# Pair-wide value products with the values as weights, in the stick-breaking and forget attentions of a three-layer transformer kernel

## The reference, cut to what matters

```python
# stick breaking, query tile i of 128 rows, keys 0..q1
z = einsum('bhqd,bhkd->bhqk', q[:, :, q0:q1], k[:, :, :q1]) * scale
strict = pos[:q1][None, :] < pos[q0:q1][:, None]
log_keep = where(strict, log_sigmoid(-z), 0.0)
log_rest = cumsum(log_keep, axis=3, reverse=True) - log_keep
a = where(strict, exp(log_sigmoid(z) + log_rest), 0.0)
out = einsum('bhqk,bhkd->bhqd', a, v[:, :, :q1])
# forget attention, the same tiles
logits = einsum('bhqd,bhkd->bhqk', q[:, :, q0:q1], k[:, :, :q1]) * scale
logits = logits + cum_log_f[:, :, q0:q1, None] - cum_log_f[:, :, None, :q1]
p = softmax(where(causal, logits, -inf), axis=-1)
out = einsum('bhqk,bhkd->bhqd', p, v[:, :, :q1])
# both: merged heads times silu(gate), then times their part of w_out
```

## Time and profile before

| what | value |
|---|---|
| median of 3 runs | 2019.23 us (2018.88 to 2021.91) |
| the profiled execution | 2014.13 us |
| its span, first to last instruction | 2012.3 us |
| PE busy | 1937.3 us, 96% of the span |
| PE weight loads busy | 1582.5 us |
| DVE / ACT / POOL busy | 773.2 / 885.8 / 661.5 us |
| mean granted PE clock | 0.992 |
| chain that ended last | PE 85%, DVE 7%, ACT 4%, issue 3% |

### The profile page before, as it was taken

The page is one execution under the profiler, slowest core; times in us unless marked ns, Lnnn a source line. Parts: engine busy times, 40 slices in busy tenths (PEclk is TensorE's granted clock), DMA queues, the critical chain, the costliest instruction groups (busy, mean ns, idle before and its releaser), DMA issues.

```text
span 2012.3 us, 25999 instructions
## 1 busy us (share of the span) xinstructions
PE 1937.3 (96%) x9707; PEld 1582.5 (79%) x9719; DVE 773.2 (38%) x1393; ACT 885.8 (44%) x1741; POOL 661.5 (33%) x278
## 2 busy tenths in 40 slices
PE   8998999999999899999999999999999999999998
PEld 6887787877788778787776788888778878888886
DVE  3435655444543565544446672010360431111002
ACT  4555565344455555534453742332453343323222
POOL 2422232321233232232122444434203424444442
PEclk9999999999999999999999999999999999999999
DMA  4221222212322122222132232223102423333232
GB/s 151 84 74 43 74 64 63 74 63 74 115 74 74 53 63 64 64 74 63 70 141 65 92 95 94 92 86 94 64 1 74 136 74 95 101 97 94 95 100 88
DMA packets 44573, 163.82 MB, mean 81 GB/s; under 512 B 6192, under 2 KB 6448, under 8 KB 43824
## 3 DMA queue, kind: packets, MB, share of 16 engines
q1 hardware_dynamic: 42640, 148.65, 23.4%
q10 hardware_dynamic: 1824, 13.63, 1.8%
HBM read 155.97 MB, written 6.29 MB: 81 GB/s over the span
## 4 chain that ended last, share of the span: by engine, by line
PE 85%; DVE 7%; ACT 4%; issue 3%; DMA 0%; POOL 0%; DVEq 0%; ACTq 0%; POOLq 0%; SPq 0%
PE bank L577 13%; PE bank L579 12%; PE bank L578 12%; PE bank L580 10%; PE bank L582 10%; PE bank L581 10%; PE bank L703 3%; PE bank L727 2%; PE bank L721 2%; PE bank L681 2%; ACT q_dup L920 1%; PE bank L682 1%; PE bank L679 1%; PE bank L723 1%; DVE y_tok L1277 1%
## 5 line engine op out<-in xcount | busy, mean ns | idle before, releaser
L560 POOL TENSOR_TENSOR w_hl<-w_raw,w_hl 128x1024 fp32r<-128x1024 f32 x274 | 661.2, 2418 | 1326.6 <-ACT w_hl L808 1326.1
L808 ACT ACTIVATE w_hl<-w_raw 128x1024 fp32r<-128x1024 f32 x274 | 287.5, 1058 | 335.2 <-DMA w_raw<-wstream 334.7
L577 PE MATMUL bank<-act_hl,w_hl 128*128 128x512 f32 x1056 | 426.8, 404 | 2.3 <-DVE act_hl L1151 1.6
L579 PE MATMUL bank<-act_hl,w_hl 128*128 128x512 f32 x1056 | 414.0, 392 | 0.0
L578 PE MATMUL bank<-act_hl,w_hl 128*128 128x512 f32 x1056 | 412.9, 391 | 0.0
L580 PE MATMUL bank<-w_hl,act_hl 128*128 128x512 f32 x672 | 265.3, 395 | 4.1 <-DVE q_low L1247 1.7
L582 PE MATMUL bank<-w_hl,act_hl 128*128 128x512 f32 x672 | 262.2, 390 | 0.0
L581 PE MATMUL bank<-w_hl,act_hl 128*128 128x512 f32 x672 | 262.1, 390 | 0.0
L577 PEld LDWEIGHTS bank<-act_hl,w_hl 128*128 128x128 f32 x1056 | 199.5, 189 | 45.1 <-DVE act_hl L1151 2.5
L579 PEld LDWEIGHTS bank<-act_hl,w_hl 128*128 128x128 f32 x1056 | 199.1, 189 | 43.3
L578 PEld LDWEIGHTS bank<-act_hl,w_hl 128*128 128x128 f32 x1056 | 199.7, 189 | 40.2 <-issue 2.2
(11 more groups left out here) (218 smaller groups left out, 2979.0 us busy)
## 6 DMA issues: line engine op xcount, KB each, us to landing
w_raw<-wstream SPq DMA_DIRECT2D x274, 512.0 KB, 3.5
x_spill<-x_res ACTq DMA_DIRECT2D x2, 2048.0 KB, 7.2
x_res<-x_spill ACTq DMA_DIRECT2D x2, 2048.0 KB, 8.1
x_res<-x SPq DMA_DIRECT2D x4, 512.0 KB, 6.2
g_post<-post_gains ACTq DMA_DIRECT2D x4, 512.0 KB, 3.7
x_res<-x ACTq DMA_DIRECT2D x1, 2048.0 KB, 7.7
out<-x_res SPq DMA_DIRECT2D x4, 512.0 KB, 2.6
probs<-w_gates ACTq DMA_DIRECT2D x1, 1024.0 KB, 9.7
```

What stands on the lines that cost most here:

```text
L560: nc.gpsimd.tensor_tensor(w_hl[:, slot, 1].rearrange("p c n -> p (c n)"), w_raw[:, slot, :], w_hl[:, slot, 0].rearrange("p c n -> p (c n)" ...
L577: pe.matmul(out_ap, wh, ah, start=start, stop=False)
L579: return pe.matmul(out_ap, wl, ah, start=False, stop=stop)
L808: nc.scalar.activation(w_hl[:, b % RING, 0].rearrange("p c n -> p (c n)"), w_raw[:, b % RING, :], ACT.Copy).then_inc(s_high_done, 1)
```

## The change

The values of a head and key block now are the weight, and the turned maps of the four query tiles of a pair are the moving operand. `pt_hl` holds both parts of both heads' maps of a whole pair: head 0's for key block k and query tile i in slot k, head 1's in slot i + 1 (`turned_part`, `turned_keys`), so that the two triangles share five slots. At steps 5, 9, 13 and 17 (`pair_turned`) `pair_values` issues for each head eight matmuls: for each of four key blocks the high and the low maps of all query tiles that see it, 512, 384, 256 and 128 columns. Head 0's stands ahead of the scores in part 0, head 1's at the end of part 1. The values lie as [high, low] for head 0 and [low, high] for head 1, so that bank BO has the main sum in the rows of the head itself and the low part in the other 64 rows. The low maps now meet both parts of the values. ACT copies the other 64 rows to the head's rows (`y_half`, 64x512), and DVE adds (`y_whole`, 64x512), which frees bank BO. Outputs then lie with features as rows, and `heads_turn` and `outputs` fall away for these two attentions. Since columns are queries now, fox rows are scaled by 1/row sum before the turning (in `inverses`), and PE's turning waits for that (`s_scaled`). ACT's first `turned` of a new pair waits for the product of the pair before with the same head, and the read-back of x waits for the last pair product. HEADS_AT moves sb's third pair to step 15 and fox's second and third to 13 and 15. The diff, cut (bookkeeping of `plan`, semaphores, `values_before`, the new order in the value drains and the removed lines of `outputs` left out):

```diff
@@ -39,7 +39,7 @@
-HEADS_AT = {"diff": (10, 13, 16, 18), "sb": (11, 13, 16, 18), "fox": (12, 14, 16, 18), "dil": (8, 13, 17, 18)}
+HEADS_AT = {"diff": (10, 13, 16, 18), "sb": (11, 13, 15, 18), "fox": (12, 13, 15, 18), "dil": (8, 13, 17, 18)}
@@ -237,6 +249,11 @@
+def pair_turned(n):
+    return n // 4 - 1 if n % 4 == 1 and n > 4 else None
@@ -272,7 +289,7 @@
     probs = at("probs", [P, 10, S], f32)
-    pt_hl = at("pt_hl", [P, 3, 2, S], f32r, probs_at + 4 * S * 4)
+    pt_hl = at("pt_hl", [P, 2, TT + 1, S], f32r, probs_at + 4 * S * 4)
@@ -282,6 +299,7 @@
     y_hl = at("y_hl", [P, 4, 2, S], f32r)
+    y_raw = at("y_raw", [P, 4, 2, S], f32, arena)
@@ -451,6 +472,24 @@
+    def turned_part(which, a, i):
+        if a == 0:
+            return pt_hl[:, which, 0:i + 1, i * P:(i + 1) * P]
+        return pt_hl[:, which, i + 1, 0:(i + 1) * P].rearrange("p (k q) -> p k q", q=P)
+    def turned_keys(which, a, kb):
+        if a == 0:
+            return pt_hl[:, which, kb, kb * P:S].rearrange("p (i q) -> p i q", q=P)
+        return pt_hl[:, which, kb + 1:TT + 1, kb * P:(kb + 1) * P]
+    def v_parts(j, high):
+        both = vhl[:, j].rearrange("p (q a) h d -> p q (a h) d", a=2)
+        return both[:, :, 0::3, :] if high else both[:, :, 1:3, :]
@@ -698,7 +739,10 @@
                 to = bank_of(("T", l, kind, n, a))
-                pe.wait_ge(*drained(("S", l, kind, n, 1 if kind == "diff" else a)))
+                if kind == "fox":
+                    pe.wait_ge(s_scaled, MARKS["scaled", (l, kind, n, a)])
+                else:
+                    pe.wait_ge(*drained(("S", l, kind, n, 1 if kind == "diff" else a)))
@@ -716,18 +760,23 @@
                         keys = slice(kb * P, (kb + 1) * P)
-                        if kind in ("sb", "fox"):
-                            v, o = vhl[:, kb, 2 * p + a], to[:, a * P:(a + 1) * P]
-                            pe.matmul(o, pt_hl[:, slot, 0, keys], v.rearrange("p h d -> p (h d)"),
-                                      start=(kb == 0), stop=False)
-                            mm = pe.matmul(o[:, HD:P], pt_hl[:, slot, 1, keys], v[:, 1, :],
-                                           start=False, stop=(kb == nb - 1))
-                            continue
...
+            def pair_values(l, kind, p, a):
+                if earlier(("O", l, kind, p, a))[1] > 0:
+                    pe.wait_ge(*earlier(("O", l, kind, p, a)))
+                pe.wait_ge(*drained(("T", l, kind, 4 * p + 3, a)))
+                for kb in range(TT):
+                    to = bank[BO][:, kb * P:S].rearrange("p (i q) -> p i q", q=P)
+                    v = vhl[:, kb, 2 * p + a].rearrange("p h d -> p (h d)")
+                    pe.matmul(to, v, turned_keys(0, a, kb), start=(kb == 0), stop=False)
+                    mm = pe.matmul(to, v, turned_keys(1, a, kb), start=False, stop=(kb == TT - 1))
+                mm.then_inc(s_pv_done, 1)
@@ -773,13 +822,15 @@
                             ready(pe, l, kind, 1)
+                        if kind in ("sb", "fox") and pair_turned(n) is not None:
+                            pair_values(l, kind, pair_turned(n), 0)
...
                             turn(l, kind, n - 1, 0)
-                        if 0 <= n - 2 < 16:
+                        if 0 <= n - 2 < 16 and kind in ("diff", "dil"):
@@ -787,7 +838,9 @@
                                 turn(l, kind, n - 1, a)
-                        if n in HEADS_AT[kind]:
+                        if kind in ("sb", "fox") and pair_turned(n) is not None:
+                            pair_values(l, kind, pair_turned(n), 1)
+                        if n in HEADS_AT[kind] and kind in ("diff", "dil"):
@@ -962,14 +1015,23 @@
                 _, nb = geometry(kind, a, row_tile(kind, n))
+                act.wait_ge(*full(("T", l, kind, n, a)))
+                ps = bank_of(("T", l, kind, n, a))[:, 0:nb * P]
+                if kind in ("sb", "fox"):
+                    if n % 4 == 0:
+                        if n > 0:
+                            act.wait_ge(s_pv_done, USE["map", l, kind, n // 4 - 1, a] + 1)
+                        elif kind == "fox":
+                            act.wait_ge(s_pv_done, USE["map", l, "sb", 3, a] + 1)
+                        else:
+                            act.wait_ge(s_pv_done, USE["map", l, "diff", 15, 0] + 1)
+                            act.wait_ge(*full(("Y", l, "diff", 3)))
+                    nc.scalar.activation(turned_part(0, a, row_tile(kind, n)), ps.rearrange("p (k q) -> p k q", q=P),
+                                         ACT.Copy).then_inc(s_p_high, 1)
+                    return
                 m = USE["map", l, kind, n, a]
-                act.wait_ge(*full(("T", l, kind, n, a)))
...
                     act.wait_ge(s_pv_done, m - 2)
-                ps = bank_of(("T", l, kind, n, a))[:, 0:nb * P]
-                if kind in ("sb", "fox"):
-                    nc.scalar.activation(pt_hl[:, m % 3, 0, 0:nb * P], ps, ACT.Copy).then_inc(s_p_high, 1)
-                    return
@@ -980,6 +1042,14 @@
+            def y_half(l, kind, p, a):
+                if p == 0 and a == 0:
+                    act.wait_ge(s_block_used, o_end(l, kind))
+                act.wait_ge(s_pv_done, USE["map", l, kind, p, a] + 1)
+                rows, other = (slice(a * HD, (a + 1) * HD) for a in (a, 1 - a))
+                nc.scalar.activation(y_raw[rows, p, 1, :], bank[BO][other, :], ACT.Copy).then_inc(s_y_half, 1)
@@ -987,9 +1057,12 @@
                 else:
-                    act.wait_ge(*drained(("Y", l, kind, p)))
+                    if kind == "diff":
+                        act.wait_ge(*drained(("Y", l, kind, p)))
+                    else:
+                        act.wait_ge(s_gated, MARKS["gated", (l, kind, p)])
                     src = y_tmp[:, :]
-                if p == 0 and (l, kind) != (0, KINDS[0]):
+                if p == 0 and kind in ("diff", "dil") and (l, kind) != (0, KINDS[0]):
@@ -1081,7 +1154,11 @@
                             row_rms(l, n - 2)
+                        if kind in ("sb", "fox") and pair_turned(n - 1) is not None:
+                            y_half(l, kind, pair_turned(n - 1), 1)
                     else:
+                        if kind in ("sb", "fox") and pair_turned(n) is not None:
+                            y_half(l, kind, pair_turned(n), 0)
@@ -1092,7 +1169,7 @@
                 elif st[0] == "xback":
-                    act.wait_ge(s_pv_done, USE["map", st[1], "fox", 15, 1] + 1)
+                    act.wait_ge(s_pv_done, USE["map", st[1], "fox", 3, 1] + 1)
@@ -1320,6 +1397,11 @@
                 link(nc.vector.reciprocal(rinv[:, n % 4, 0:2], sums[:, par, 0:2]))
+                if kind == "fox":
+                    for a in range(2):
+                        _, nb = geometry(kind, a, row_tile(kind, n))
+                        row = probs[:, p_slot(kind, n, a), 0:nb * P]
+                        nc.vector.tensor_scalar(row, row, rinv[:, n % 4, a:a + 1], None, ALU.mult).then_inc(s_scaled, 1)
@@ -1331,14 +1413,15 @@
                 _, nb = geometry(kind, a, row_tile(kind, n))
-                m = USE["map", l, kind, n, a]
...
                     dve.wait_ge(s_p_high, MARKS["p_high", (l, kind, n, a)])
-                    nc.vector.tensor_tensor(pt_hl[:, m % 3, 1, 0:nb * P], ps, pt_hl[:, m % 3, 0, 0:nb * P].bitcast(f32),
-                                            ALU.subtract).then_inc(done, 1)
+                    i = row_tile(kind, n)
+                    nc.vector.tensor_tensor(turned_part(1, a, i), ps.rearrange("p (k q) -> p k q", q=P),
+                                            turned_part(0, a, i).bitcast(f32), ALU.subtract).then_inc(done, 1)
                     return
+                m = USE["map", l, kind, n, a]
@@ -1355,21 +1438,34 @@
                     return
-                if kind == "dil":
-                    nc.vector.tensor_scalar(dst, o[:, 0:P], rinv[:, n % 4, 0:1], None, ALU.mult).then_inc(done, 1)
+                nc.vector.tensor_scalar(dst, o[:, 0:P], rinv[:, n % 4, 0:1], None, ALU.mult).then_inc(done, 1)
+            def y_whole(l, kind, p, a):
+                rows = slice(a * HD, (a + 1) * HD)
+                dve.wait_ge(s_y_half, MARKS["y_half", (l, kind, p, a)])
+                raw = y_raw[rows, p, 1, :]
+                link(nc.vector.tensor_tensor(raw, bank[BO][rows, :], raw, ALU.add))
+                dve.sem_inc(freed(("O", l, kind, p, a)), 1)
+            def gated(l, kind, p):
+                if p == 0:
+                    for done_tile in group_drained(group("g", l=l, kind=kind)):
+                        dve.wait_ge(*done_tile)
+                nc.vector.tensor_tensor(y_tmp[:, :], y_raw[:, p, 1, :], gate[:, p, :], ALU.mult)\
+                    .then_inc(s_gated, 1)
+                dve.wait_ge(s_gated, MARKS["gated", (l, kind, p)])
+                dve.wait_ge(s_y_high, MARKS["y_high", (l, kind, p)])
```

(31 more changed lines are left out.)

24 lines of the change are left out of this document (8 added, 16 removed).

## The result

The changed kernel takes 2030.3 us (median of five runs, 2029.4 to 2035.2); the kernel before, run beside it, 2019.2. The ratio is 1.0065, 95% interval [1.0052, 1.0078]: slower by 13 us, against 17 forecast. The profiled execution took 2035.16 us.

A forecast was written before the change was run, and what follows sets the result against it. PE, busy 96% of the span, was taken to bound the kernel. Per layer -19.2 + 6.7 + 2.2 + 8.35 + 7.65 = +5.7 us, twice +11.4, clock +6, put on the median: 2036 us; range 2004 to 2052.

The forecast's parts named there:

- The direct saving: PE, both attentions: value matmuls and head turns removed, pair products of 1.27 us added; net -19.2 us per layer.
- half speed: Rival: head 1's maps, read in pieces of 128 columns, stream at half rate on PE; +20 us, 2056; chance 0.04.
- The wait behind the sticks: Steps 5, 9, 13: PE's head 1 product waits for y_whole behind DVE's sticks; 6.7 us per layer, forget attention 2.2.
- Savings that existing waits swallow: Drains and late steps of both attentions: where PE already waits, less PE work only lengthens the wait; 8.35 us per layer.
- The forget tail: S(12) to first output product: ACT and DVE chain lengthens; 30.7 us, 5.1 later than before, or 7.65 given back per layer.
- The sum without the clock: Whole kernel: direct saving, new waits, swallowed savings and tail added up; +5.7 us per layer, +11.4 for two.
- The clock: PE in both attentions: more waits bring four more stretches at the lower clock; +6 us, ends 0 and +20.
- The number, 2036: Whole kernel: +17.4 us on the profiled execution's 2014.1, then put on the median of the runs; 2036 us.
- forecast case: Whole kernel slower: 2020 to 2050 us, also given as 2022 to 2050, likeliest 2036; chance 0.67.
- the tail (31 forecast: Sign named beforehand: forget tail near 31 us if right, no longer than 26 us if wrong.
- the 25 that would have spoken for the rival: Sign against the forecast: PE's waits in the attentions under 25 us in all, so the rival stands.
- saving survives: Rival: slack of ACT and DVE in drains and tail keeps PE's saving; -6.5 us per layer, 2009; chance 0.21.

The follow-up runs named there:

- e_fill: Changed kernel with head 1's four transposes ahead of the y_whole waits in stick-breaking steps 5, 9 and 13 made five times; ratio to the kernel before 1.0049.
- e_front: Changed kernel with head 0's y_half moved ahead of sigmoids and exponentials on ACT, y_whole ahead of sticks or scalings on DVE; ratio to the kernel before 0.9950.
- e_noscale: Changed kernel without the scaling of the forget attention's rows by 1/sum, so part of the result is not computed; ratio to the kernel before 1.0061.
- e_front_tail: e_front with head 1's maps of the forget attention's last four rows transposed into bank 1, not head 0's bank; ratio to the kernel before 0.9946.

## Why the prediction was right, point by point

The side was right, the range held it, and the number (2036) was 6 us above. By its own steps:

- **The direct saving, -19.2 us per layer:** the prices of the new products are confirmed, the saving was too high. A product took 1.34 us behind a wait (252.92 to 254.26) against 1.27, and head 1's 128-column pieces cost nothing, so "half speed" is out. Up to S(12) the forecast has 16.7 of the 19.2. In stages without a stretch PE's busy time falls from 152.4 to 144.4 in stick breaking (e_fill's 149.8 less 48 repeated transposes at 0.112) and from 92.9 to 86.8 in the forget attention, 14.1 together. The missing 2.6 I cannot place in single rows.
- **The wait behind the sticks, 3 x 2.2 us:** there, 1.97 each, at steps 5, 9 and 13 in both layers. In the forget attention 0.95 against 1.1. All twelve come to 17.9 us where I had said some 18, but that match is luck: my terms were 2 x (6.7 + 2.2) = 17.8 us without the tail, and 2.3 of the 17.9 are in the tail (2 x 1.14 in step 13). e_front showed by removal that they are on the path.
- **Savings that existing waits swallow, 8.35 per layer:** the mechanism held, the size was a little high. Against before, PE waits 1.2 more in the drain of sb step 7 (0.99 and 0.54, where 0.34 stood; 1.55 forecast) and 1.5 at the gates of step 10 (1.24 and 0.27, where none stood; 1.7 forecast). In steps 14 and 15 it waits 3.72 where 0.87 and 1.82 stood; its profiled execution has a stretch there, and without one 1.51 more are waited for T(14,0) (e_fill, layer 1), so 2.5 (2.4 forecast). Forget step 7 waits 2.96 plus 0.66 where 2.51 stood ("near 4" forecast), step 11 2.36 against 1.10. Sum 1.2 + 1.5 + 2.5 + 1.1 + 1.3 = 7.6. These two rows of PE, both in layer 0, are the largest:
```profile
337.92 0.58 PE L621 MATMUL bank<-w_hl,act_hl 128*128 128x512 f32 x1 [3.72 <-DVE q_low L1324]
...
433.01 0.44 PE L747 MATMUL bank<-ident,probs 128*128 128x128 f32 x2 [2.96 <-DVE pt_hl L1421]
```
- **The forget tail, +5.1:** S(12) to the first output product took 33.4 us (467.17 to 500.60), where the hand schedule had 30.7. From S(14) on it held: 19.3 us to the output product, 18.9 forecast. The 2.3 before S(14) (14.1 against 11.8) fall partly into a stretch of 6.8 us from 467.8 on, that my schedule did not have; with half of it (e_fill) S(14) comes at 13.2. The window lies between 29.3 and 32.8 at full clock, against 25.6 before: +3.7 to +7.2. The two reasons that were tried cost little by themselves: the scaling (e_noscale) and the shared turning bank (e_front_tail).
- **The sum without the clock, +5.7 per layer:** 5.2 to 8.7 by the stages without a stretch (see the result). For stick breaking alone my terms give -9.6 + 6.7 + 5.65 = +2.75, and 158.7 against 155.4 is +3.3. Up to S(12) the saving was 2.6 us too high and the waits 1.9 (15.4 against 17.25), so two errors nearly cancel there.
- **The clock, +6:** four stretches more were forecast. Within the two attentions the profiled executions have 10 us at the lower level before and 41 after, nine stretches' worth more. At 1.6 us for each that would be 15 us, but the one in stick-breaking step 14 costs nothing, and in the tail 3.4 us more of it cost 0.6 (33.4 against 32.8 in e_fill). What is left of the 19.9 us between the profiled executions, after 2 x 5.2 to 8.7 for the rest, is 2.5 to 9.5 us: the 6 lies inside.
- **The number, 2036 for 2030.3:** the sum was compared with a quick execution and then put on the median, as if the median execution had no more stretches than the profiled one. It has: the clock was 0.990 on average against 0.992. Between the profiled executions the clock differs by 0.009, on average by 0.005. There, as far as the runs tell, the excess lies; in a single stretch it cannot be shown. (My forecast case is given once as 2020 to 2050 and once as 2022 to 2050; nothing hangs on it.)

Of the signs named beforehand, the tail (31 forecast, 33.4 found) was the least exact, and PE's waits in the attentions, 54.6 us idle in both layers, are far from the 25 that would have spoken for the rival. The rival "saving survives" had its reason in slack at the drains and in the tail. e_front is faster than before by 10 us, but not for that reason: its drains wait as long and its tail is as long as in the changed kernel, and what went are the waits for y_whole. **Left open:** why the forget attention is still 2.1 and 3.6 us longer than before with e_front's order. Scaling, the shared bank, the padding and the form of the last pair were each changed, and none alone gave it back. The lower clock has up to 6.8 us of the 33.5 in e_front's tail, but what of it is on the chain was not tried, and no tail at full clock was seen with pair products.

## What to carry to other kernels

When two products share an accumulator bank, the operation that empties it is on the path of the second one: place it in its engine's program by who waits for it, not beside the work of its own stage. Here that alone turned a loss of 0.0065 into a gain of 0.0050. Before a stretch at the lower clock is priced, look whether a wait for another engine behind it would have taken the time anyway. Make larger, rarer products where other work follows to cover the two copies behind them; where a stage ends in a bare chain, test it without them first.

## What the runs showed of the hardware

- Waits of PE of 1.97 us in stick breaking were followed by a stretch at 1.2 GHz in seven of eight stages at one place and in one of sixteen at the two other places; with the waits filled by repeated transposes no stretch came there in two stages. At its price of 1.6 us a wait of 2 us can cost 3.6.
- A stretch of 3.4 us cost 1.6 us where PE set the pace, and nothing where PE would have waited 1.51 us for DVE's split behind it (e_fill, 158.66 us with and 158.73 without).
- The moving operand of a matmul (f32), read as up to four pieces of 128 columns, 512 columns apart, streams like a contiguous one (480.29 to 480.53: 0.24 us for 512 columns, against 0.23 in the dense products).
- 40 matmuls without use in a tail with gaps cost no time (33.5 and 33.7 us with and without) and held the clock at 0.80 instead of 0.69 (layer 0 of one execution each).
